# Expert loop in twelve steps of four 32-row blocks, 96 rows for each expert, and the overflow loop between two per-layer products

## What is computed

```python
    u = rmsnorm(h, norm_ffn)
    ...
    in_grp = jnp.take_along_axis(exp_logits, grp[..., None, None], axis=2)[..., 0, :]
    top_v, top_i = lax.top_k(in_grp, TOP_K)
    w_top = jax.nn.softmax(top_v, axis=-1) * p_grp
    expert_id = grp[..., None] * EXPERTS_PER_GROUP + top_i
    ...
    for e in range(N_EXPERTS):
        gu = jnp.einsum('bld,df->blf', u, w_gate_up[e])
        hid = jax.nn.silu(gu[..., :D_EXPERT]) * gu[..., D_EXPERT:]
        moe = moe + combine[..., e:e + 1] * jnp.einsum('blf,fd->bld', hid, w_down[e])
    h = h + moe

    u = rmsnorm(h, norm_ple)
    gate = jax.nn.sigmoid(jnp.einsum('bld,de->ble', u, w_ple_gate))
    h = h + gate * jnp.einsum('blp,pd->bld', p_l, w_ple_proj)
```

## Time and profile before

| | us |
|---|---|
| median of 3 runs | 873.87 |
| lowest and highest | 873.84, 874.2 |
| span of the profiled execution | 872.5 |
| first gate/up product of the loop starts | 597.0 |
| last down product ends | 780.8 |
| first combining gather starts | 786.6 |

### The profile page before, as it was taken

How to read it: one execution, slowest core, us unless ns; L and a number is a source line. 1 busy time by engine, 2 the same in 40 slices (tenths; PEclk the granted TensorE clock), 3 DMA queues, 4 the chain that set the end, 5 groups by cost and what they waited for, 6 DMA issues and landing times.

```text
span 872.5 us, 11853 instructions
## 1 busy us (share of the span) xinstructions
PE 854.9 (98%) x4645; PEld 556.1 (64%) x4645; DVE 388.7 (45%) x857; ACT 223.3 (26%) x478; POOL 155.1 (18%) x186
## 2 busy tenths in 40 slices
PE   8999999999999999999999999999999999999996
PEld 4546777888799877777777764565444444444452
DVE  3223566677546324566734577364211111104553
ACT  2202152265224210121011101230311111125454
POOL 0324420022243314201300250002000000003000
PEclk9999999999999999999999999999999999999998
DMA  9521343502020201334132221157999999685211
GB/s 362 188 85 65 134 124 134 151 1 105 1 99 3 98 1 44 163 111 150 55 139 96 97 97 76 49 193 276 393 373 371 367 365 371 251 319 169 71 38 48
DMA packets 19814, 135.98 MB, mean 156 GB/s; under 512 B 2512, under 2 KB 3024, under 8 KB 12592
## 3 DMA queue, kind: packets, MB, share of 16 engines
q1 hardware_dynamic: 12176, 103.28, 30.9%
q0 software_dynamic: 5424, 26.45, 8.7%
q10 hardware_dynamic: 2160, 5.51, 2.1%
HBM read 117.83 MB, written 21.60 MB: 160 GB/s over the span
## 4 chain that ended last, share of the span: by engine, by line
PE 43%; DVE 3%; issue 2%; ACT 1%; DMA 1%; POOLq 0%; POOL 0%; DVEq 0%; ACTq 0%
PE single L1250 13%; PE pair L1234 6%; PE pair L1151 6%; PE single L914 6%; PE pair L1352 3%; PE pair L935 2%; PE single L1222 2%; PE pair L1290 2%; PE single L935 2%; PE single L1199 1%; DMA mem<-y_slots,posu 1%; PE single L1160 1%; DVE mem L2322 0%; PE single L1263 0%; DVE mem L2082 0%
## 5 line engine op out<-in xcount | busy, mean ns | idle before, releaser
L734 PE MATMUL pair<-mem 128*128 128x288 f32 x640 | 158.9, 408 | 0.0
L734 PEld LDWEIGHTS pair<-mem 128*128 128x128 f32 x640 | 120.3, 190 | 35.6 <-ACT mem L1373 2.1
L1250 PE MATMUL single<-mem 128*128 128x512 f32 x256 | 112.8, 593 | 0.8 <-DVE mem L2284 0.8
L914 PE MATMUL single<-mem 128*128 128x288 f32 x448 | 110.0, 407 | 0.3
L914 PEld LDWEIGHTS single<-mem 128*128 128x128 f32 x448 | 84.7, 190 | 25.7 <-issue 1.6
L1250 PEld LDWEIGHTS single<-mem 128*128 128x128 f32 x256 | 47.3, 190 | 54.1 <-issue 53.1
L1373 ACT ACTIVATE mem<-single 128x256 f32<-128x256 f32 (+5 forms) x113 | 46.5, 421 | 133.2 <-PE single L1160 48.7
L1373 ACT ACTIVATE mem<-pair 128x512 f32<-128x512 f32 (+5 forms) x85 | 37.8, 495 | 164.0 <-PE pair L734 63.1
L2277 DVE SCALAR_TENSOR_TENSOR mem<-single,mem 128x256 f32<-128x256 f32 x16 | 7.7, 483 | 138.8 <-PE single L1250 126.3
L1352 PE MATMUL pair<-mem 128*128 128x512 f32 (+1 forms) x192 | 63.4, 524 | 1.1 <-DVE mem L2332 1.1
L1234 PE MATMUL pair<-mem 128*128 128x512 f32 x128 | 57.7, 593 | 0.5 <-ACT mem L1373 0.5
(11 more groups left out here) (394 smaller groups left out, 1152.3 us busy)
## 6 DMA issues: line engine op xcount, KB each, us to landing
mem<-in_w_gu SPq DMA_DIRECT2D x16, 2048.0 KB, 9.1
mem<-in_w_down SPq DMA_DIRECT2D x16, 1024.0 KB, 11.8
y_slots<-mem SPq DMA_DIRECT2D x16, 512.0 KB, 3.7
y_slots<-in_zeros POOLq DMA_DIRECT2D x8, 512.0 KB, 8.4
mem<-in_w_ga SPq DMA_DIRECT2D x2, 2048.0 KB, 8.6
mem<-in_w_gb SPq DMA_DIRECT2D x2, 2048.0 KB, 8.4
mem<-in_w_wo SPq DMA_DIRECT2D x2, 2048.0 KB, 8.1
mem<-in_w_pg SPq DMA_DIRECT2D x2, 2048.0 KB, 11.5
```

Source lines behind the costliest of these rows:

```text
L734: last = nc.tensor.matmul(pb[:, hf, 0:HALF], w(k), rhs[:, k, hf * HALF:(hf + 1) * HALF], start=(k == 0), stop=(k == kk - 1))
L914: last = nc.tensor.matmul(single[plan.buf[s]][:, 0:HALF], lhs[:, k, :], rhs[:, k, :], start=(k == 0 and j in (0, 1, 3, 4)), stop=(k == 3), ...
L1250: last = nc.tensor.matmul(single[3][:, :], xT[u % 2][:, k, :], w_gu[u][:, k, :], start=(k == 0), stop=(k == KD - 1))
```

## The change

The 1536 regular slots become 96 for each expert (`CAP`), and a step of the loop (`p`, 12 of them) takes 128 consecutive slots: four blocks of 32, each of which belongs to one expert (`blocks_of`). A step's gate/up product is, for each of 8 contraction slices, four products with 32 rows of `xT`, each with its own expert's weights, into four partition ranges of `single3`; the down product is cut in the same way. Three blocks of four steps share an expert's weights, so a step uses two or three experts' weights. SP fetches gate/up weights as soon as the last gate/up product that reads the old ones is done, and down weights one step later, behind the store; the two have semaphores of their own. `w_proj` and the two halves of `w_pg` move to the end of the loop, the second half behind the overflow weights.

The steps `ovp` and `idv` go. What they did is done in the loop: DVE makes the tables in step 0, PE one list of ten products of 64 columns in step 1, and DVE the table of blocks. The overflow loop takes blocks of 32 rows, up to 32 of them, past 96 rows of an expert. It uses all four column groups by splitting the output's columns (gate/up 4 x 128, down 4 x 256), stands between the second and the third per-layer product, has its rows gathered early, and its result is stored by four transfers on ACT's queue. POOL starts the combining gathers only when it has left that loop. With the rows above the loop runs once, for the two last rows of expert 1.

```diff
 NCONV = 12
 NG, NE_G, NEXP, DE = 4, 4, 16, 256
-NOV = 8
-SLOTS = (NEXP + NOV) * P
+CAP, BS = 96, 32
+NPH = NEXP * CAP // P
+NOV = 32
+SLOTS = NEXP * CAP + NOV * BS
...
+def blocks_of(p):
+    return [((4 * p + g) // 3, (4 * p + g) % 3, g) for g in range(4)]
...
+def last_phase(e):
+    return (3 * e + 2) // 4
...
-            def after_expert(e, u, more):
-                sp.wait_ge(sem("y_ready"), 2 * e + 2)
-                sp.dma_start(y_slots[bass.ds(e * P, P), :], yb[u % 2]).then_inc(sem(f"y_stored{u % 2}"), 16)
-                if more:
-                    sp.dma_start(w_gu_flat[u], a["w_gu"][bass.ds((e + 4) * P, P), :]).then_inc(sem(f"wgu{u}"), 16)
-                    sp.dma_start(w_dn_flat[u], a["w_down"][bass.ds((e + 4) * P, P), :]).then_inc(sem(f"wgu{u}"), 16)
...
+            def store(p):
+                sp.wait_ge(sem("y_ready"), 2 * p + 2)
+                sp.dma_start(y_slots[p * P:p * P + P, :], yb[p % 2]).then_inc(sem(f"y_stored{p % 2}"), 16)
+            for p in range(NPH - 1):
+                sp.wait_ge(sem("gu_mm"), p + 1)
+                for e in range(NEXP - 4):
+                    if last_phase(e) == p:
+                        load_gu(e + 4)
+                if p == NPH - 2:
+                    sp.dma_start(view(BLK, CHUNK_W), a["w_pg0"]).then_inc(sem("w_pg"), 16)
+                if p:
+                    store(p - 1)
+                for e in range(NEXP - 4):
+                    if last_phase(e) == p - 1:
+                        load_dn(e + 4)
+                if p == NPH - 3:
+                    sp.dma_start(w_proj.rearrange("p k c -> p (k c)"), a["w_proj"]).then_inc(sem("w_proj"), 16)
+            sp.wait_ge(sem("ov_ready"), 3)
...
-                    sp.dma_start(w_gu_flat[3], a["w_gu"][bass.ds(e * P, P), :]).then_inc(sem("ov_w"), 16)
-                    sp.dma_start(w_dn_flat[3], a["w_down"][bass.ds(e * P, P), :]).then_inc(sem("ov_w"), 16)
-                    sp.wait_ge(sem("ov_act"), 4 * i + 4)
-                    sp.dma_start(y_slots[bass.ds((i + NEXP) * P, P), :], yb[0]).then_inc(sem("ov_stored"), 16)
-                    sp.wait_ge(sem("ov_stored"), 16 * i + 16)
-                    sp.sem_inc(sem("ov_free"), 1)
-            for b in range(2):
-                sp.wait_ge(sem(f"y_stored{b}"), 16 * 8)
-            sp.sem_inc(sem("y_all"), 1)
+                    sp.dma_start(w_gu_flat[0], a["w_gu"][bass.ds(e * P, P), :]).then_inc(sem("ov_w"), 16)
+                    sp.dma_start(w_dn_flat[0], a["w_down"][bass.ds(e * P, P), :]).then_inc(sem("ov_w"), 16)
+            store(NPH - 2)
+            sp.wait_ge(sem("gu_mm"), NPH)
+            sp.dma_start(view(BLK + 12288, CHUNK_W), a["w_pg1"]).then_inc(sem("w_pg"), 16)
+            store(NPH - 1)
...
+            def down(p):
+                pe.wait_ge(sem("hT"), p + 1)
+                for e in experts_of(p):
+                    pe.wait_ge(sem(f"wdn{e % 4}"), 16 * (e // 4 + 1))
+                if p >= 2:
+                    pe.wait_ge(sem("y_ready"), 2 * p - 2)
+                if p == 1:
+                    pe.wait_ge(sem("ov_ready"), 3)
                 for n in range(2):
                     for k in range(2):
-                        last = nc.tensor.matmul(pair[u % 2][:, n, :], hT[u % 2][:, k, :], w_dn[u][:, k, n * 512:(n + 1) * 512],
-                                                start=(k == 0), stop=(k == 1))
+                        for e, _, g in blocks_of(p):
+                            last = nc.tensor.matmul(pair[p % 2][BS * g:BS * g + BS, n, :], hT[p % 2][:, k, BS * g:BS * g + BS],
+                                                    w_dn[e % 4][:, k, n * 512:(n + 1) * 512], start=(k == 0), stop=(k == 1))
                 last.then_inc(sem("dn_mm"), 1)
 
...
+            xpose(0)
+            for p in range(NPH):
+                pe.wait_ge(sem("xT" if p else "xT_half"), p + 1)
+                for e in experts_of(p):
+                    pe.wait_ge(sem(f"wgu{e % 4}"), 16 * (e // 4 + 1))
+                if p:
+                    pe.wait_ge(sem("hid"), p)
                 for k in range(KD):
-                    if first and u == 0 and k == 4:
-                        pe.wait_ge(sem("xT"), 1)
-                    last = nc.tensor.matmul(single[3][:, :], xT[u % 2][:, k, :], w_gu[u][:, k, :],
-                                            start=(k == 0), stop=(k == KD - 1))
-                    if first and u == 0 and k == 3:
-                        xpose(xg_next[0], e + 1, u + 1)
+                    if p == 0 and k == 4:
+                        xpose(1)
+                    for e, _, g in blocks_of(p):
+                        last = nc.tensor.matmul(single[3][BS * g:BS * g + BS, :], xT[p % 2][:, k, BS * g:BS * g + BS],
+                                                w_gu[e % 4][:, k, :], start=(k == 0), stop=(k == KD - 1))
                 last.then_inc(sem("gu_mm"), 1)
-                if nxt and not (first and u == 0):
-                    xpose(xg_next[0], e + 1, u + 1)
...
                                                     w_proj[:, k, hf * 512 + cols.start:hf * 512 + cols.stop], start=(k == 0), stop=(k == 1))
                 last.then_inc(sem("pp_mm"), 1)
 
-            for t in range(NT - 1):
+            for t in range(2):
                 p_product(t)
 
-            pe.wait_ge(sem("ov_ready"), 1)
-            pe.wait_ge(sem("y_ready"), 32)
-            n_ov = pe.value_load(ovi[0:1, 2 * NOV:2 * NOV + 1], min_val=0, max_val=NOV)
-            pe.wait_ge(sem("dn_mm"), 16)
-            pe.wait_ge(sem("pp_mm"), NT - 1)
-            pe.sem_inc(sem("ov_free"), 1)
+            pe.wait_ge(sem("ov_ready"), 3)
+            n_ov = pe.value_load(ovi[0:1, NOV:NOV + 1], min_val=0, max_val=NOV)
             with pe.If(n_ov > 0):
                 with pe.Fori(0, n_ov) as i:
                     pe.wait_ge(sem("ov_xg"), 16 * i + 16)
+                    pe.sem_inc(sem("ov_turn"), 1)
                     for k in range(KD):
-                        out = single[k // 4][:, (k % 4) * P:(k % 4 + 1) * P]
-                        last = nc.tensor.transpose(out, xg[0][:, k * P:(k + 1) * P], C("ident"))
+                        last = nc.tensor.transpose(single[0][:, BS * k:BS * k + BS], xg_ov[:, k * P:(k + 1) * P], C("ident")[0:BS, 0:BS])
                     last.then_inc(sem("ov_pe"), 1)
                     pe.wait_ge(sem("ov_dve"), 2 * i + 1)
                     pe.wait_ge(sem("ov_w"), 32 * i + 32)
                     for k in range(KD):
-                        last = nc.tensor.matmul(single[3][:, :], xT[0][:, k, :], w_gu[3][:, k, :],
-                                                start=(k == 0), stop=(k == KD - 1))
+                        for g in range(4):
+                            last = nc.tensor.matmul(single[3][BS * g:BS * g + BS, 0:P], xT_ov[:, k, :], w_gu[0][:, k, P * g:P * g + P],
+                                                    start=(k == 0), stop=(k == KD - 1))
                     last.then_inc(sem("ov_pe"), 1)
                     pe.wait_ge(sem("ov_dve"), 2 * i + 2)
+                    pe.sem_inc(sem("ov_turn"), 1)
+                    nc.tensor.transpose(single[2][:, 0:64], hid_ov, C("ident")[0:64, 0:64]).then_inc(sem("ov_pe"), 1)
+                    pe.wait_ge(sem("ov_act"), 3 * i + 2)
                     for k in range(2):
-                        last = nc.tensor.transpose(single[2][:, k * P:(k + 1) * P], hid[0][:, k * P:(k + 1) * P], C("ident"))
+                        for g in range(4):
+                            last = nc.tensor.matmul(single[1][BS * g:BS * g + BS, 0:DE], hT_ov[:, BS * k:BS * k + BS],
+                                                    w_dn[0][:, k, DE * g:DE * g + DE], start=(k == 0), stop=(k == 1))
                     last.then_inc(sem("ov_pe"), 1)
-                    pe.wait_ge(sem("ov_act"), 4 * i + 2)
-                    pe.wait_ge(sem("pp"), NT - 1)
-                    for n in range(2):
-                        for k in range(2):
-                            last = nc.tensor.matmul(pair[0][:, n, :], hT[0][:, k, :], w_dn[3][:, k, n * 512:(n + 1) * 512],
-                                                    start=(k == 0), stop=(k == 1))
-                    last.then_inc(sem("ov_pe"), 1)
...
+            for p in range(NPH):
+                expert_act(p)
+                if p == 1:
                     act.wait_ge(sem("rt_exp"), 1)
                     nc.scalar.activation(rt[:, 1, :, :], rt[:, 0, :, :], ACT.Exp)
                     nc.scalar.activation(rs[:, 1, :], rs[:, 0, :], ACT.Exp).then_inc(sem("rt_act"), 1)
-            y_evac(1, 16, 16 * 7)
+            y_evac((NPH - 1) % 2, NPH, 16 * ((NPH - 1) // 2))
+            act.wait_ge(sem("ov_ready"), 3)
+            n_ov = act.value_load(ovi[0:1, NOV:NOV + 1], min_val=0, max_val=NOV)
+            with act.If(n_ov > 0):
+                with act.Fori(0, n_ov) as i:
+                    act.wait_ge(sem("ov_pe"), 4 * i + 2)
```

(35 more changed lines are left out.)

357 lines of the change are left out of this document (162 added, 195 removed).

## The result

The changed kernel takes **851.43 us** (median of 4 runs, 849.67 to 851.74) against 874.04 us beside it (873.84 to 875.23): a ratio of **0.9732**, 95% interval 0.9715 to 0.9748. The forecast was 857.2 us with a range of 848 to 869. The profiled execution has a span of 849.3 us and a time of 851.12.

What follows compares the result with a forecast made beforehand. The matrix engine was taken to bound the kernel, with DMA engines near their limit in the expert loop. A first combining gather 17.9 us earlier plus 1.2 for the clock gave -16.7, span 855.8, time 857.2 us, range 848 to 869.

Steps and rivals of the forecast that it cites:

- Four groups together, -45.6 us: Expert loop on PE: four 32-column products cost one full instruction, so 12 steps replace 16 at 11.39 us, -45.6 us.
- Rivals 1 and 2: Loop products: packing costs more per round, 866 us, 7%; or only two of four groups run at once, 964 us, 5%.
- Hence a step costs PE what an expert costs, 11.39 us: Expert loop: a step of four packed blocks takes PE as long as one expert did, 11.39 us.
- ids product, +1.1: Behind step 1's transposes: ten 64-column products, 20 instructions at half the old cost, add some 1.1 us.
- Early ids steps and split copies at 0, between -1 and +0.5: Before the loop: dropping two early ids steps and splitting the ids copies together cost 0, between -1 and +0.5 us.
- The DMA wall, +12.3 us before step 9: Expert loop: a full queue at 395 GB/s lands expert 13's weights about 711, so PE waits 12.3 us by step 9.
- rival 3: Expert loop: no DMA wall, deeper queues reach 460 GB/s, last down product 736.3, time 840 us; chance 5%.
- Last down product 748.6: End of the expert loop: the last down product ends at 748.6 us, against 736.3 by PE alone.
- The first two per-layer products (3.4 us, from 13.9/4): After the loop: two per-layer products take 3.4 us and end at 752, before the overflow weights land at 755.
- The overflow loop: After the loop: one pass for expert 1's 98 rows, starting at 755, 11.5 us long, rows in memory at 766.7.
- my third sign: Tail: wrong if the gather stands over 3 us behind the overflow store or the last ordinary store is later than it.
- The tail, 1.2 us for the clock: After the gather: the old tail, plus 1.2 us (range 0 to 3) for PE's first transposes at the low clock.

Runs made afterwards that it cites:

- e1: Changed kernel with row transposes moved behind the small ones and made two steps ahead, two tile-width changes a step instead of four: 850.33 us, ratio 0.9723.
- e4: Changed kernel without the second half of the contraction of every down product, all transfers kept: 847.8 us, ratio 0.9695.
- e5: Changed kernel without the loop for rows past 96 and its loads: 844.6 us, ratio 0.9663.
- the four tail kernels: e7, e9, e11 and e12: changed kernel with e1's transposes, overflow loop right behind the last down product, differing in SP's order at the end: 849.78 to 853.88 us.
- e8: Kernel before the change, with half a megabyte more to load for each of experts 4 to 15: 875.31 us beside 875.13, ratio 1.0002.
- e6: Changed kernel with gate/up products issued four contraction slices of one block in a row, then the next block: 959.21 us, a single run.
- e7: Changed kernel with e1's transposes, overflow loop right behind the last down product, its weights loaded ahead of per-layer input and gate weights: 851.85 us, ratio 0.9731.
- e10: The changed kernel run again, unchanged: 850.96 us, ratio 0.9719.
- e9: As e7, with the last ordinary store issued ahead of the second half of the gate weights: 853.88 us, ratio 0.977.
- e11: As e7, but overflow gate/up weights loaded earlier and the second half of the gate weights only after the first per-layer product: 849.78 us, ratio 0.9704.
- e12: As e11, with the second half of the gate weights issued right behind the last ordinary store: 852.9 us, ratio 0.9736.

## Why the prediction was right, and where it was not

- **Four groups together, -45.6 us.** Right: 7.09 us of busy time a step, and no excess at 512 columns. By the prediction's own sign (8 us or more) this step holds. Rivals 1 and 2 are out, and so is the 2.38 times of the Trainium skill ("TensorE: Matmul & The Clock Gate", Part 3) for these fp32 products: the measured round of four starts every 0.43 us like one full-width product, so the measurement decides.
- **"Hence a step costs PE what an expert costs, 11.39 us".** Wrong by 0.58 us a step, some 6 us in all (5.2 over the nine steps from 2 to 11, the rest around them). The step of the reasoning that failed is that I summed the products and not the borders between them. The rows of L900 and L795 were 2.4 and 2.2 us where eight rounds give 1.98; I put all of that down to the end of a burst, and whether a border is part of it was not asked.
- **ids product, +1.1.** It took 2.5 us, 1.4 more: 0.125 for each of its 20 instructions of 64 columns, as much as one of the 128 columns of before (1.50/12): half the columns did not halve it.
- **Early ids steps and split copies at 0, between -1 and +0.5.** 0.46, inside; the fall of the clock in that execution added 1.27.
- **The DMA wall, +12.3 us before step 9.** It was 0: "PE has no wait before step 9" was my own sign that the second step is wrong. "I count bytes ... at 395, between those rows" is what failed: the rate was 422 GB/s, and I had read a busy share of 0.95 at 368 as a full queue, though the earlier trace rows has 424. The sum had a slip besides: 598.5 + 44 MB at 395 is 709.9, not 711 (and 755 and 726 stand 0.8 and 1.4 us too high in the same way). With 44 MB at 422 the landing is 598.5 + 104 = 702.8, and 706.4 was measured; PE came at 707.3, 8.7 us later than the 698.6 of the forecast. Had PE kept the pitch of 11.39 from step 2 on, it would have come some 3 us before the weights; e1 and e4 show the wall there. So rival 3 was right that no wait comes, though not by its 460 GB/s and not in its time.
- **Last down product 748.6.** Measured 746.2. PE by itself was to end at 736.3 and came 9.9 us later: 6.3 for the borders, 1.4 for the ids product, 2.25 for the late start. The queue was to add 12.3 and added nothing. These errors have opposite signs and almost cancelled, so that this figure came out is luck.
- **"The first two per-layer products (3.4 us, from 13.9/4)".** A misreading: 13.9 us is four products, so 3.4 is one, and two took 7.06 (746.13 to 753.19). With it PE would have come at 755.6 in my sum, and not at 752 ahead of the weights. It did come last, at 753.2.
- **The overflow loop.** It ran once, as said, but without waiting for weights (issued 734.96, 16.0 us to landing, so there at 751.0; PE came at 753.2), and it took 9.7 us from its first transposes to the landing of its rows (last issue at 761.4, 1.5 us) against 11.5. The granted clock fell at 760.9, behind its last product. e5 prices it at 6.6 us of the end.
- **The last ordinary store, 763.** It landed at 758.4 (issued 747.38, 11.0 us), and the overflow store decided, as forecast; the gather went out 1.9 us behind it, inside the 3 of my third sign.
- **The tail, 1.2 us for the clock.** The clock was low from 760.9 to 767.7, and the two products of L1304 took 9.46 for 7.13 us. But the first transposes behind them waited for VectorE anyway, by 0.41 us, so it cost nothing. In e5 and the four tail kernels, where TensorE stood idle instead, it cost 1.4 to 2.6 us.

The sum was -16.7, the span changed by -23.2. Of the 6.5 between them 1.8 are the start of the overflow loop (755 forecast, 753.2 measured), 2.0 its length to the landing (766.7 forecast, 762.9 measured), 0.1 the way to the gather (768.7 and 764.8), 1.2 the clock, and 1.4 a tail that is shorter from the gather on (84.5 us, 85.9 before), which the runs did not take apart. The range and the direction were right, and so were the packing and the overflow loop; that the time came within 6 us owes something to luck, since the loop's end did.

## What to carry to other kernels

A busy share near 1 does not say that a queue is full: compare its GB/s with the best stretch of the trace, and if the share is below 1 ask whether it runs empty between bursts; a small extra load, as in e8, tests it. When products are packed into column groups, count the changes of tile width in a loop body and order the body so that they are few. A gain in a loop that fills the queue can be partly given back behind it (here 12.5 of 34.6 us), where the next stage's small stores stand behind the loads that were issued ahead of need. And before moving work out of a wait of the matrix engine, look at what follows the wait: here the idle stretch that it left was followed by products at the low clock.

## What the runs showed of the hardware

- A change between 32-wide products and 128-wide transposes costs TensorE 0.15 us (steps of 11.67, 11.97 and 12.26 us with two, four and six changes).
- The DMA engines of one core kept 416 to 427 GB/s (422 on average) from 610 to 735 us, with gathers and stores of 4 KB rows among weight rows of 8 and 16 KB. The Trainium skill gives 425 as measured for a load of 16 MB and 435 as the ceiling ("DMA: Bandwidth & Descriptors", Where 436 GB/s comes from), and the trace agrees with both. The same section says that transfers between HBM and SBUF are bound at about 358; with one core at work the trace is above that, and the measurement decides.
- Packed products issued block by block, eight instructions of one column group in a row, run two at a time (15.85 us for 64), slice by slice four (7.07).
- The granted clock fell to 0.5 for 3.4 us in the router stretch in two of eleven executions of the same instructions, and by the traces' clock records it first rose between 4.3 and 11.1 us after the start. Where it rose after 10 us (e6, e7, e10) the first gate/up product stands at 600.0 to 601.1, in the others at 597.5 to 599.2: single traces differ by up to 3.6 us there without a cause in the kernel.
- After TensorE had idled 3.2 to 5.8 us ahead of the first gate transposes, the granted clock was 0.5 at their start or within 0.6 us of it, and the way from them to the gate product took 4.3 to 5.5 us and not 2.9 (e5, e7, e9, e11, e12).
